# The first mixer's projections with tokens on the partitions, and its heads with projection pieces between their steps

## The reference

```python
a_q, a_k, a_v, b_ql, b_kvl, b_kr = split_cols(h @ w_in, AB_IN_SPLITS)
a_q = rope(rms_norm(a_q.reshape(B, S, 2 * A_HEADS, A_QK_DIM), a_q_norm), pos)
a_k = rope(rms_norm(a_k.reshape(B, S, 2 * A_HEADS, A_QK_DIM), a_k_norm), pos)
out_a = differential_attention(a_q[:, :, :, 0], a_q[:, :, :, 1], a_k[:, :, :, 0], a_k[:, :, :, 1], a_v, lam, A_QK_DIM ** -0.5)
out_a = rms_norm(out_a, a_out_norm) * (1.0 - lam_0)
q_b = (rms_norm(b_ql, b_q_a_norm) @ b_w_q_b)
kv_b = (rms_norm(b_kvl, b_kv_a_norm) @ b_w_kv_b)
out_b = latent_attention(q_nope, q_rope, k_nope, k_rope, b_v, (B_NOPE_DIM + B_ROPE_DIM) ** -0.5)
return mixed @ w_out
```

## Time and profile before

| what | us |
|---|---|
| median of 3 runs | 1469.23 (1468.61 to 1469.86) |
| the profiled execution | 1467.24 |
| its span in the trace | 1465.4 |
| TensorE, matmul records | 1394.1 (95%) |
| TensorE, weight loads beside them | 1136.8 (78%) |
| VectorE | 645.9 (44%) |
| ScalarE | 572.4 (39%) |
| GpSimd | 549.0 (37%) |
| mean granted clock of TensorE | 0.962 |

### The profile page before, as it was taken

One profiled execution on the slowest core, in us unless ns is written; L12 is line 12 of the kernel. 1 busy time (PEld: TensorE's weight loads), 2 busy tenths in 40 slices (PEclk: granted clock), 3 DMA queues, 4 the chain that ended last, 5 costly groups with the idle time before them and its releaser, 6 DMA issues.

```text
span 1465.4 us, 17999 instructions
## 1 busy us (share of the span) xinstructions
PE 1394.1 (95%) x6564; PEld 1136.8 (78%) x6564; DVE 645.9 (44%) x1168; ACT 572.4 (39%) x959; POOL 549.0 (37%) x249
## 2 busy tenths in 40 slices
PE   6979888999899999999999899999899999999999
PEld 4767777888678888888887788888678888888887
DVE  5466676666632220122243778888623221022210
ACT  4233334554433231222233677777533232122220
POOL 5222231232463444334463321222164435334351
PEclk9978887888999999999999999999999999999999
DMA  5111110010122232232321211111032232222330
GB/s 205 58 44 35 38 33 13 24 34 1 56 98 102 86 126 87 76 100 86 117 86 56 71 59 43 43 57 57 30 101 83 90 117 99 72 90 97 113 124 36
DMA packets 29718, 107.73 MB, mean 74 GB/s; under 512 B 3424, under 2 KB 3680, under 8 KB 29664
## 3 DMA queue, kind: packets, MB, share of 16 engines
q1 hardware_dynamic: 29520, 106.97, 21.9%
q10 hardware_dynamic: 144, 0.02, 0.0%
HBM read 104.88 MB, written 2.10 MB: 73 GB/s over the span
## 4 chain that ended last, share of the span: by engine, by line
PE 71%; issue 10%; DVE 9%; ACT 8%; POOL 2%; DMA 0%; ACTq 0%; DVEq 0%; POOLq 0%; SPq 0%
PE bank L290 19%; PE bank L286 19%; PE bank L287 19%; PE bank L638 2%; POOL w_lo L274 2%; DVE cs_hi L1074 2%; PE bank L368 1%; ACT ca L1032 1%; ACT w_hi L262 1%; PE bank L433 1%; DVE cs_lo L1076 1%; ACT ca L1030 1%; PE bank L723 1%; DVE h_lo L383 1%; PE bank L895 1%
## 5 line engine op out<-in xcount | busy, mean ns | idle before, releaser
L274 POOL TENSOR_TENSOR w_lo<-wraw,w_hi 128x1024 fp32r<-128x1024 f32 (+2 forms) x176 | 450.7, 2562 | 710.3 <-ACT w_hi L262 710.3
L286 PE MATMUL bank<-h_hi,w_hi 128*128 128x512 f32 x1024 | 414.8, 405 | 17.7 <-DVE h_lo L383 11.5
L287 PE MATMUL bank<-h_lo,w_hi 128*128 128x512 f32 x1024 | 408.8, 399 | 0.0
L262 ACT ACTIVATE w_hi<-wraw 128x1024 fp32r<-128x1024 f32 (+2 forms) x176 | 193.9, 1102 | 256.1 <-DVE x L606 171.4
L290 PE MATMUL bank<-h_hi,w_lo 128*128 128x512 f32 x1024 | 260.4, 396 | 0.0
L286 PEld LDWEIGHTS bank<-h_hi,w_hi 128*128 128x128 f32 x1024 | 196.1, 192 | 69.5 <-DVE h_lo L383 17.9
L287 PEld LDWEIGHTS bank<-h_lo,w_hi 128*128 128x128 f32 x1024 | 196.1, 192 | 44.3 <-issue 1.0
L290 PEld LDWEIGHTS bank<-h_hi,w_lo 128*128 128x128 f32 x1024 | 194.0, 189 | 45.5
L287 PE MATMUL bank<-f_lo,w_hi 128*128 128x512 f32 x352 | 138.9, 395 | 0.0
L286 PE MATMUL bank<-f_hi,w_hi 128*128 128x512 f32 x352 | 138.9, 395 | 0.0
L592 DVE TENSOR_TENSOR fu<-bank,rstd 128x512 f32<-128x512 f32 x44 | 30.4, 691 | 203.9 <-PE bank L290 203.9
(11 more groups left out here) (222 smaller groups left out, 1997.7 us busy)
## 6 DMA issues: line engine op xcount, KB each, us to landing
wraw<-in_w_in SPq DMA_DIRECT2D x141, 512.0 KB, 3.3
wraw<-in_w_down SPq DMA_DIRECT2D x32, 704.0 KB, 4.1
bwraw<-in_w_b SPq DMA_DIRECT2D x6, 416.0 KB, 3.2
x<-in_xt SPq DMA_DIRECT2D x8, 256.0 KB, 4.9
out<-x SPq DMA_DIRECT2D x8, 256.0 KB, 2.2
wraw<-in_w_in SPq DMA_DIRECT2D x3, 256.0 KB, 4.2
tabb<-in_tabs_b SPq DMA_DIRECT2D x1, 512.0 KB, 8.3
taba<-in_tabs_a SPq DMA_DIRECT2D x1, 512.0 KB, 9.1
```

What stands on the lines that cost most here:

```text
L262: nc.scalar.activation(whi[:, s, 0:width], wraw[:, s, 0:width], ACT.Copy).then_inc(S("w_hi"), 1)
L274: nc.gpsimd.tensor_tensor(wlo[:, s, 0:width], wraw[:, s, 0:width], whi[:, s, 0:width], ALU.subtract).then_inc(S("w_lo"), 1)
L286: nc.tensor.matmul(out_bank, w, src_hi[kt], start=(kt == 0), stop=False)
L287: nc.tensor.matmul(out_bank, w, src_lo[kt], start=False, stop=False)
```

## The change

The mixer of layer 0 is written anew; the rest keeps its instructions, apart from norm and weight split, which change places in `out_act`, `ffn_act` and GpSimd's program.

- Projections hold a tile of 128 features x 128 tokens of `h` in the array and move weights: 416 columns of latents (`lat_pe`), 384 and 512 of B's queries and of its keys and values (`bq_pe`, `bkv_pe`), 256 of A's (`pj_pe`). Results have tokens on the partitions and heads along the free axis.
- Norms are squares on ScalarE and `reduce_sum` on VectorE over the free axis; the root is a scalar per partition. Rotation is done by products with a table on VectorE (`qk_dve`, `b_pair_dve`), its sum for A on GpSimd. Fixed matrices other than identity and ones are gone. A's queries are not normed, their root is the scale of the exponential.
- Query and key of a head are transposed back by TensorE ahead of the scores (`b_qk_pe`, `a_qk_pe`, eight transposes a head).
- B's heads come first. `pj_pe` pieces (12 matmuls of 256 columns) of A's groups stand between their steps, four a head. In A's heads stand two `ob_pe` halves, the output projection of B's results. `oa_pe`, that of A's results, comes last.
- Scores of a head lie in banks 0 to 2, and its transposed probabilities come back into the same banks.
- The sum of squares of the first norm moves from GpSimd to VectorE; ten matmuls on zeros stand at the start.

```diff
+G_B = 6
+G_PJ = (4, 10, 12, 14, 16, 18)
+G_OB = 20
+G_OA = 24
...
+    def norm_sum_dve(dve, n, d):
+        if d == 0:
+            return
+        dve.wait_ge(*at_norm(n, "sq", d + 1))
+        if d > 1:
+            dve.wait_ge(*at_norm(n, "sum", d - 1))
+        nc.vector.tensor_tensor(ssum[:], sqn[:, 0, :] if d == 1 else ssum[:], sqn[:, d % 2, :],
+                                ALU.add).then_inc(S("norm_sum"), 1)
...
+    def lat_pe(pe):
+        for kt in range(KT):
+            g, k = kt // 2, kt % 2
+            c = slice(k * LAT, (k + 1) * LAT)
+            pe.wait_ge(*at_norm(0, "lo", kt + 1))
+            if k == 0:
+                pe.wait_ge(S("w_hi"), g + 1)
+            if kt < KT - 1:
+                for i in range(NB):
+                    nc.tensor.matmul(bank[i][:, 0:LAT], tok(hhi, kt, i), whi[:, slot(g), c], start=(kt == 0), stop=False)
+                    nc.tensor.matmul(bank[i][:, 0:LAT], tok(hlo, kt, i), whi[:, slot(g), c], start=False, stop=False)
+                if k == 0:
+                    pe.wait_ge(S("w_lo"), g + 1)
+                for i in range(NB):
...
+    def bq_pe(pe, hf, i):
+        g, n = G_B + 2 * hf, NB * hf + i
+        if i == 0:
+            pe.wait_ge(S("w_lo"), g + 1)
+            pe.wait_ge(S("l_lo"), 2)
+        if n >= 2:
+            pe.wait_ge(S("bq_sq"), n - 1)
+        o = bank[i % 2][:, 0:BQ_N]
+        for k in range(2):
+            c = slice(k * BQ_N, (k + 1) * BQ_N)
+            nc.tensor.matmul(o, tok(qlhi, k, i), whi[:, slot(g), c], start=(k == 0), stop=False)
+            nc.tensor.matmul(o, tok(qllo, k, i), whi[:, slot(g), c], start=False, stop=False)
+            last = nc.tensor.matmul(o, tok(qlhi, k, i), wlo[:, slot(g), c], start=False, stop=(k == 1))
+        last.then_inc(S("bq" if i < NB - 1 else "chunk_done"), 1)
...
+    def bkv_dve(dve, hf, i):
+        n = NB * hf + i
+        b = bank[KV_BANK[n % 3]]
+        dve.wait_ge(S("bk_sq"), n + 1)
+        nc.vector.tensor_copy(kb[:, 4 * hf:4 * hf + 4, i, :],
+                              b[:, 0:256].rearrange("p (h n) -> p h n", h=4)).then_inc(S("bk_ev"), 1)
+        c = slice(256 * hf, 256 * hf + 256)
+        nc.vector.tensor_tensor(vblo[:, i, c], b[:, 256:512], vbhi[:, i, c], ALU.subtract).then_inc(S("bv_lo"), 1)
+        nc.vector.reduce_sum(tiny[:, T_BS + 48 * hf + 16 + i:T_BS + 48 * hf + 32:NB], bk_sq[:, i % 2, :].rearrange("p (h n) -> p h n", h=4),
+                             AX).then_inc(S("bk_sum"), 1)
...
+    def b_pair_dve(dve, pr):
+        hf, h, z = pr // 2, 2 * pr, Z_B[pr // 2] + 8 * (pr % 2)
+        dve.wait_ge(S("rs_root"), ROOT[f"b{hf}"] + 1)
+        dve.wait_ge(S("bq_ev"), NB * hf + NB)
+        dve.wait_ge(S("bk_ev"), NB * hf + NB)
+        q = qb[:, h:h + 2, :, :]
+        s, c = B_ROPE // 2, B_NOPE
...
+    def pj_pe(pe, p, c, i):
+        g = G_PJ[p] + c
+        if i == 0:
+            pe.wait_ge(S("w_lo"), g + 1)
+        if c == 0 and p > 0 and i % 2 == 0:
+            if p <= 4:
+                pe.wait_ge(S("pj_c"), 2 * (p - 1) + i // 2 + 1)
+            else:
+                pe.wait_ge(S("va_lo"), NB * (p - 5) + i + 2)
+        o = pj_of(i)
+        for k in range(4):
+            w = slice(256 * k, 256 * k + 256)
+            nc.tensor.matmul(o, tok(hhi, 4 * c + k, i), whi[:, slot(g), w], start=(c == 0 and k == 0 and i % 2 == 0),
+                             stop=False, skip_group_check=True)
+            nc.tensor.matmul(o, tok(hlo, 4 * c + k, i), whi[:, slot(g), w], start=False, stop=False,
+                             skip_group_check=True)
+            last = nc.tensor.matmul(o, tok(hhi, 4 * c + k, i), wlo[:, slot(g), w], start=False,
+                                    stop=(c == 1 and k == 3), skip_group_check=True)
+        if i == NB - 1:
+            last.then_inc(S("chunk_done"), 1)
+        elif c == 1 and i == 1:
+            last.then_inc(S("pj"), 1)
...
+    def qk_dve(dve, p, t):
...
+        nc.vector.tensor_tensor(u[:, :, :, 0:s], y[:, :, :, s:2 * s], of(A_DIM, s), ALU.mult)
+        nc.vector.tensor_tensor(u[:, :, :, s:2 * s], y[:, :, :, 0:s], of(A_DIM + s, s), ALU.mult)
+        nc.vector.tensor_tensor(o, y, of(0, A_DIM), ALU.mult).then_inc(S("pj_c"), 1)
+        nc.vector.reduce_sum(col(T_AS + 16 * p + 8 * t, 8), pj_sq[:].rearrange("p (j n) -> p j n", n=A_DIM),
+                             AX).then_inc(S("pj_sum"), 1)
...
+    def pt_trans_pe(pe):
+        for c, blocks in enumerate((((0, 0), (1, 0), (2, 0), (3, 0)), ((1, 1), (2, 1), (3, 1)), ((3, 3), (2, 2), (3, 2)))):
+            for n, (b, kb) in enumerate(blocks):
+                at = (4 - len(blocks) + n) * P
+                last = nc.tensor.transpose(bank[c][:, at:at + P], pn[:, PO[b] + kb * P:PO[b] + (kb + 1) * P], M["ident"])
+            last.then_inc(S("h_t"), 1)
...
+    def b_scores_pe(pe, u):
+        pe.wait_ge(S("h_qlo"), u + 1)
+        pe.wait_ge(S("h_klo"), u + 1)
+        if u == 0:
+            pe.wait_ge(S("kr_lo"), 1)
+        else:
+            pe.wait_ge(S("h_plo"), 3 * u)
...
+    def a_scores_pe(pe, u, b):
...
+            if b == 3:
+                pe.wait_ge(*at_a("e", 8 * u + 2 * j + 2))
...
+    def ob_pe(pe, u, e):
+        g = G_OB + u
+        pe.wait_ge(S("w_lo"), g + 1)
+        if u == 0 and e == 0:
+            pe.wait_ge(S("h_mlo"), B_HEADS)
+            pe.wait_ge(S("va_lo"), 2 * NB)
+        else:
+            pe.wait_ge(S("ob_x"), 2 * u + e)
+        for k in range(4):
+            last = out_step_pe(g, e, bank[7][:], k, A_HEADS, k == 0, k == 3)
+        last.then_inc(S("chunk_done" if e else "ob"), 1)
...
-    def b_sums_pe(pe, u):
-        pe.wait_ge(*at_head("b", "qsq", u + 1))
-        pe.wait_ge(*at_head("b", "ksq", u + 1))
-        q2, k2 = b_squares(u)
-        for i in range(NB):
-            c = slice(i * P, (i + 1) * P)
-            nc.tensor.matmul(bank[MMB][:, 3 * i:3 * i + 2], q2[0:B_QK, c], M["blk_b"][0:B_QK, 0:128:64],
-                             start=True, stop=True)
-            last = nc.tensor.matmul(bank[MMB][:, 3 * i + 2:3 * i + 3], k2[0:B_NOPE, c],
-                                    M["blk_b"][0:B_NOPE, 0:1], start=True, stop=True)
-        last.then_inc(S("rs_sum"), 1)
...
-            def b_pe(u, n, s):
-                if n:
-                    pe.wait_ge(*at_head("b", "qs", u + 1))
-                    b_sums_pe(pe, u + 1)
-                for b in range(NB):
-                    scores_pe(pe, "b", u, b)
-                if n:
-                    rs_spread_pe(pe, rs_b(u + 1), 2, MMB, step=3)
-                    pe.wait_ge(*at_head("b", "e", u * NB + 2))
-                    b_spread_k_pe(pe, u + 1)
-                else:
...
+            def keep_busy(n):
+                for _ in range(n):
+                    nc.tensor.matmul(bank[7][:], zeros[:, 0:P], zeros[:, 0:SEQ], start=True, stop=True)
+            pe.wait_ge(S("zeros"), 1)
+            keep_busy(10)
+            lat_pe(pe)
...
+            for u in range(B_HEADS):
+                p, c = 2 + u // 2, u % 2
+                b_scores_pe(pe, u)
+                if u < B_HEADS - 1:
+                    b_qk_pe(pe, u + 1)
+                else:
+                    a_qk_pe(pe, 0)
+                pj_pe(pe, p, c, 0)
+                pj_pe(pe, p, c, 1)
+                b_ptrans_pe(pe, u)
+                pj_pe(pe, p, c, 2)
+                b_values_pe(pe, u, 0)
+                pj_pe(pe, p, c, 3)
+                for kb in range(1, NB):
+                    b_values_pe(pe, u, kb)
+            for u in range(A_HEADS):
+                a_scores_pe(pe, u, 0)
+                a_scores_pe(pe, u, 1)
+                if u:
                     a_osum_pe(pe, u - 1)
+                a_scores_pe(pe, u, 2)
+                a_scores_pe(pe, u, 3)
+                if u:
+                    a_ospread_pe(pe, u - 1)
+                ob_pe(pe, u, 0)
+                if u < A_HEADS - 1:
+                    a_qk_pe(pe, u + 1)
+                a_ptrans_pe(pe, u)
+                ob_pe(pe, u, 1)
+                for kb in range(NB):
+                    a_values_pe(pe, u, kb)
             u = A_HEADS - 1
+            oa_pe(pe, 0, range(u))
             a_osum_pe(pe, u)
...
```

More of the change, by code:

```diff
@@ new lines, in trunk @@
+    assert end <= r0 + 4 * SEQ
+    qa, _ = place("qa", [P, 2, NB, 4 * A_DIM], F32, at=phase0)
+    ka, _ = place("ka", [P, 2, NB, 4 * A_DIM], F32, at=phase0 + half)
+    vsize = 4 * NB * 2 * P
+    kb0 = q0 + 4 * B_HEADS * NB * B_QK
+    vahi = [place(f"va{n}_hi", [P, NB, 2 * P], F32R, at=at)[0] for n, at in enumerate((q0, q0 + vsize))]
+    valo = [place(f"va{n}_lo", [P, NB, 2 * P], F32R, at=at)[0] for n, at in enumerate((kb0, q0 + 2 * vsize))]
+    (akhi, aklo), end = pair("ak", [P, SEQ], at=bq0)
@@ new lines, in a_values_pe @@
+    def a_values_pe(pe, u, kb):
+        pe.wait_ge(*at_a("plo", 3 * u + min(kb + 1, 3)))
+        if kb == 0:
+            if u == 0:
+                pe.wait_ge(S("h_mlo"), B_HEADS)
+            else:
+                pe.wait_ge(S("a_og"), u)
```

(10 more changed lines are left out.)

1788 lines of the change are left out of this document (925 added, 863 removed).

## The result

| | before | after |
|---|---|---|
| median, us | 1468.93 (1468.61 to 1469.86, 4 runs) | 1354.22 (1351.68 to 1355.07, 4 runs) |
| profiled execution, its span | 1467.24, 1465.4 | 1355.07, 1353.2 |

The account below looks back on a forecast made before the run. TensorE's program was taken to bound the kernel. Stages ending at 26, 80, 192, 268 and 292 us put the mixer's end at 292 instead of 413.3, 121 less: 1467.2 - 121 = 1346, range 1318 to 1380.

Parts of the forecast that it names:

- What bounds, what goes: Mixer to 413 us: TensorE's program is the bound; sums, spreads and rotations go, net 63 us less TensorE work.
- Start, 26 us: Latent projection: ends at 26 us in the worst case, VectorE losing all 8 us beside GpSimd.
- Prologue, 80: From 26 us to the first scores: mostly bounded by VectorE, scores at about 80 us, TensorE having 40 us of work.
- root 0.8: Prologue, VectorE's chain behind the first key/value half: the root takes 0.8 us.
- B heads, 12.2 us of TensorE each and 13.4 extra: Eight B heads, 80 to 192 us: 8 x 12.2 of TensorE plus 13.4 of VectorE work in the chain, 111 us.
- so I charge only instructions with two SBUF inputs: VectorE beside GpSimd: only instructions with two SBUF inputs lose time; a two-port scaling, 354 ns mean, does not.
- A heads, 19 each: Four A heads, to 268 us: TensorE 15.8, waits 1.2 and clock loss 1.1 among the terms, 76 us in all.
- Behind the mixer, 0 with bounds of 3: Behind 413 us: norm before weight split at three transitions gains 0, bounds -3 and +3; granted clock already 0.99.
- Rival 1: Mixer: VectorE's order becomes the bound, B heads 15 us, A heads 21.5, prologue 15 more; time 1379; chance 0.18.
- Rival 2: 26 to 268 us: the clock stays low at 0.86, costing 33 us instead of 4; time 1372; chance 0.15.
- Rival 4: Heads: shared banks 0 to 2 make them serial, B head 26 us, A 38; slower, time 1533; chance 0.05.
- Rival 5: B heads: pieces' weights come late, showing as small waits within rival 1; chance 0.18 for both together.

Follow-up runs that it names:

- pieces_last: The changed kernel with the four projection pieces of each B head behind its values instead of between its steps; 1383.8 us.
- prologue: The changed kernel with chunk 10's high part made earlier on ScalarE and chunk 11's low part on GpSimd only behind the first pair's rotation; 1352.17 us.
- hold: The changed kernel with twelve matmuls on zeros added behind the sums of the first norm; 1352.4 us.
- final: The changed kernel with the edits of windows, prologue and hold, A groups' second-half evacuations one head earlier, and q0's first half ahead of the latents' evacuation; 1317.53 us.
- windows: The changed kernel with GpSimd's work in the heads waiting until it lies beside VectorE's evacuations from PSUM; 1340.32 us.
- before_pad: The kernel before with 192 unused bytes per partition ahead of the normed input's buffers, no instruction changed; 1455.4 us.
- before_norm_first: The kernel before with the norm ahead of the weight split at the three transitions; 1462.38 us.
- after_split_first: The changed kernel with the old order, weight split ahead of norm, at the three transitions; 1359.27 us.

## Why the prediction was right and where it was not

The total, 1354 against 1346, hides two errors of opposite sign: +19.0 us in the mixer and -9.9 behind it. That they nearly cancel is luck; with the mixer's error alone it would have been 1364, still in the range and 18 us off.

- **What bounds, what goes.** Right as far as the runs tell. With the sums, spreads and rotations gone and the pieces in a poor order, pieces_last still ends the mixer 73 us earlier. No run took these matmuls out alone, so their share is an estimate. Of the 102 us that the mixer lost, the prediction's 63 are TensorE's work. Some 29 are the clock: 99 us at half speed between 26 and 413.3 before, 41 between 25.4 and 311 now, half of the difference. Two are waits: 46.5 before, 44.3 now. That is 94 of 102. The forecast counted on shorter waits as well, and they did not get shorter.
- **Start, 26 us.** 25.3. The worst case for VectorE was not reached; TensorE waited 0.3 us for `h_lo`.
- **Prologue, 80.** 89.8, and three causes with 3.2 (prologue), 2.5 (hold) and 3.4 us (final, first scores from 85.6 to 79.6 less hold's 2.5) make up 9.1 of the 9.8 (each read from one profiled execution, and sure to 1 or 2 us only; together they are sure, 79.6 in final). The step that failed first was "root 0.8": two of its four steps took 4.6 us beside GpSimd. Next, the fall of the clock behind the wait for chunk 4: I had the wait, to 29.8, but priced the pieces behind it at full speed. Last, ScalarE's wait for VectorE's sum of q0's first half, 4.0 us, ahead of all of B's queries.
- **B heads, 12.2 us of TensorE each and 13.4 extra.** TensorE's 12.2 was right: heads with nothing in the way take 12.0. The extra was 121.6 - 97.6 = 24, not 13.4. The term that failed is the sentence "so I charge only instructions with two SBUF inputs": it priced the pair's block at 3 x 1.4 and the roots at nothing. In the trace each of the three blocks lost 4.4 us to two GpSimd instructions, and four roots 2 us each. Windows took this away and gave 110.9. That this is the forecast's 111 is partly luck: heads 1, 3 and 5, behind the pair's block, then take 12.0 where 1.4 each was charged, and heads 2 and 4 exceed 12.2 by 4.8 and 3.2 where 2.2 each was. The reading under the charge was wrong too. I had taken from L691's mean of 354 ns that a product with a scalar does not wait for GpSimd. But none of the 32 instructions of L691 ran beside a GpSimd instruction, and the trace of the kernel before had small ones that did, a step of a root with 2.96 us and a product with a scalar with 1.55, where the shortest of their kinds take 0.16:

```profile
67.33 2.96 DVE L352 TENSOR_TENSOR tiny<-tiny 128x8 f32<-128x8 f32 x1 [0.51 <-ACT tiny L347]
67.86 2.40 POOL L274 TENSOR_TENSOR w_lo<-wraw,w_hi 128x1024 fp32r<-128x1024 f32 x1
...
143.06 1.55 DVE L660 TENSOR_SCALAR tiny<-tiny 128x2 f32<-128x2 f32 x1
142.21 2.37 POOL L274 TENSOR_TENSOR w_lo<-wraw,w_hi 128x1024 fp32r<-128x1024 f32 x1 [17.05 <-ACT w_hi L262]
```

- **A heads, 19 each.** 75.8 against 76, by luck. The first took 22.7, with waits and a fallen clock; the others 17.7, without the waits and the clock loss that I had put into each.
- **Output, 24.** 23.8.
- **Behind the mixer, 0 with bounds of 3.** -9.9. The pace of the matmuls gives -8.5 (before_pad), the order of norm and split -2.1 behind the network's first matmul (before_norm_first) and up to -5.3 (after_split_first), and the first network starts worse than before by 3.4. Together these are -7.2 to -10.4. The 3.4 can be read in the two traces: a wait of 2.3 us for GpSimd's sum (L375 at 320.32) that was not there before, then six matmuls 0.43 us apart instead of 0.23 while the clock is low (321.96 to 324.09), 1.7 us with those around them, less 0.7 of a wait for `h_lo` that got shorter. Why the sum comes late was not tried. The 8.5 are luck: nobody had chosen the place of the buffers. The reason that I gave for 0, a granted clock of 0.99 there, says nothing on the 4.9 us of waits for `h_lo`, and I had read the waits up to 410 us only. The placement no row of the kernel before could have shown.
- **Rival 1, VectorE's order, 0.18.** In the B heads it happened: 15.2 us a head where it assumed 15; in the A heads not.
- **Rival 2, the clock.** 0.93 from 26 to 311 us and not 0.86. In the B heads it falls three times, in heads 2, 4 and 7, close to where TensorE stood 3.9, 3.7 and 2.2 us for the scaling, and in no head with a shorter stand. A stand does not always bring a fall: head 6 stood 2.4 us without one, and in windows heads 2 and 4 stood 3.2 us each and only head 2's clock fell. In final every head but the last has 18 transposes, the longest stand is 2.2 us, and the clock is 1.00: the rule of the Trainium skill on transposes that I weighed (TensorE: Matmul & The Clock Gate, Part 4) did not bear on these.
- **Rival 4, serial heads.** Even with the pieces put last a head takes 19.1 us, not 26: the banks were a threat only on paper. **Rival 5:** no wait for a weight part in any head.
